# Gated linear attention block: the gates' chain ahead of four silus and of the values' units, an output unit's half made ahead, and the join of the sums of squares inside the last tile

## What is computed

```python
q, k, v, r, lr = jnp.split(hn @ w_in, [...], axis=-1)
gk = jax.nn.log_sigmoid((lr @ w_gate + b_gate)) / GLA_TAU        # TAU = 16
bcum = jnp.cumsum(chunks(padf(gk), GLA_DK), axis=3)
q_dec, k_dec = qf * jnp.exp(bcum), kf * jnp.exp(-bcum)
att = jnp.where(causal, einsum(q_dec, k_dec), 0.0)
chunk_kv = einsum(kf * jnp.exp(b_last - bcum), vf)
o = att @ vf + q_dec @ states
o = rmsnorm(o, g_head) * jax.nn.silu(r)
mix = o @ w_out
h = h + rmsnorm(mix, g[3])
```

## Time and profile before

| | us |
|---|---|
| median of 3 runs (1863.05 to 1868.45) | 1863.25 |
| the profiled execution, its own time | 1867.49 |
| its span in the profile | 1865.7 |
| TensorE busy / weight loads | 1772.6 / 1466.3 |
| VectorE busy | 1092.7 |
| ScalarE busy | 723.7 |
| mean granted TensorE clock | 0.975 of full |

### The profile page before, as it was taken

How to read it: one execution, slowest core, us unless ns; L and a number is a source line. 1 busy time by engine, 2 the same in 40 slices (tenths; PEclk the granted TensorE clock), 3 DMA queues, 4 the chain that set the end, 5 groups by cost and what they waited for, 6 DMA issues and landing times.

```text
span 1865.7 us, 33049 instructions
## 1 busy us (share of the span) xinstructions
PE 1772.6 (95%) x12810; PEld 1466.3 (79%) x12810; DVE 1092.7 (59%) x1981; ACT 723.7 (39%) x1196; POOL 25.1 (1%) x33
## 2 busy tenths in 40 slices
PE   8999998979999999998999999997989999999995
PEld 7999987879999899997899999997954444444442
DVE  4676456578775777669787756868753223232323
ACT  5334453354444544444654446855321111111111
POOL 1000000000000000000000001000002000000000
PEclk8999998989999999999999999998999999999998
DMA  6545422224554355532245545442579999999994
GB/s 222 159 173 200 161 91 94 88 91 158 180 193 168 115 180 183 215 143 91 86 141 182 207 176 190 148 159 91 203 315 416 420 421 420 420 421 420 421 420 200
DMA packets 55534, 409.62 MB, mean 220 GB/s; under 512 B 6432, under 2 KB 6432, under 8 KB 7968
## 3 DMA queue, kind: packets, MB, share of 16 engines
q1 hardware_dynamic: 53424, 401.69, 56.5%
q0 software_dynamic: 1744, 5.79, 1.1%
q10 hardware_dynamic: 288, 1.05, 0.1%
HBM read 405.87 MB, written 2.63 MB: 219 GB/s over the span
## 4 chain that ended last, share of the span: by engine, by line
PE 77%; DVE 11%; DMA 7%; ACT 3%; issue 1%; SPq 0%; DVEq 0%; ACTq 0%
PE ps L565 77%; DMA ring<-w_gate_up 6%; DVE w_lo L1544 1%; ACT moe L1473 1%; PE ps L569 1%; DVE h L1650 1%; DMA raw<-w_units 1%; DVE x_lo L1606 1%; DVE h L1654 1%; DVE arena L1902 1%; DVE rs L1586 1%; DVE arena L1930 0%; ACT w_hi L1167 0%; DVE small L1908 0%; DVE arena L1827 0%
## 5 line engine op out<-in xcount | busy, mean ns | idle before, releaser
L565 PE MATMUL ps<-x_hi,w_hi 128*128 128x256 f32 (+1 forms) x2144 | 622.6, 290 | 17.6 <-DVE x_lo L1604 8.2
L565 PE MATMUL ps<-x_lo,w_hi 128*128 128x256 f32 (+1 forms) x2144 | 616.2, 287 | 0.0
L565 PE MATMUL ps<-x_hi,w_lo 128*128 128x256 f32 (+1 forms) x2144 | 614.2, 286 | 0.0
L1544 DVE TENSOR_TENSOR w_lo<-raw,w_hi 128x1024 fp32r<-128x1024 f32 (+1 forms) x352 | 440.9, 1291 | 86.1 <-ACT w_hi L1167 85.7
L565 PEld LDWEIGHTS ps<-x_hi,w_hi 128*128 128x128 f32 x2144 | 409.5, 191 | 29.1 <-issue 13.7
L1167 ACT ACTIVATE w_hi<-raw 128x1024 fp32r<-128x1024 f32 (+1 forms) x352 | 378.6, 1111 | 110.5 <-PE ps L565 87.2
L565 PEld LDWEIGHTS ps<-x_hi,w_lo 128*128 128x128 f32 x2144 | 411.4, 192 | 0.0
L565 PEld LDWEIGHTS ps<-x_lo,w_hi 128*128 128x128 f32 x2144 | 410.7, 192 | 0.2
L565 PE MATMUL ps<-ring,moe 128*64 128x512 f32 x1536 | 340.4, 595 | 6.4 <-DMA ring<-w_gate_up 4.6
L565 PEld LDWEIGHTS ps<-ring,moe 128*64 128x64 f32 x1536 | 106.0, 137 | 215.8 <-issue 188.6
L565 PE MATMUL ps<-hid_hi,w_hi 128*128 128x272 f32 (+1 forms) x720 | 206.0, 286 | 0.7 <-DVE hid_lo L1606 0.3
(11 more groups left out here) (310 smaller groups left out, 1806.5 us busy)
## 6 DMA issues: line engine op xcount, KB each, us to landing
raw<-w_units SPq DMA_DIRECT2D x144, 1024.0 KB, 4.8
ring<-w_gate_up SPq DMA_DIRECT2D x128, 1024.0 KB, 19.6
ring<-w_down SPq DMA_DIRECT2D x64, 1024.0 KB, 18.4
raw<-w_out_units SPq DMA_DIRECT2D x32, 1408.0 KB, 6.1
bias_rows<-arena POOLq DMA_DIRECT2D x8, 192.0 KB, 3.6
cst<-table SPq DMA_DIRECT2D x1, 1448.0 KB, 12.9
h<-xT SPq DMA_DIRECT2D x1, 1088.0 KB, 5.0
arena<-bias_rows POOLq DMA_DIRECT2D x8, 128.0 KB, 2.5
```

What stands on the lines that cost most here:

```text
L565: return nc.tensor.matmul(out_ap, lhsT, rhs, start=start, stop=stop, skip_group_check=True)
L1544: v.tensor_tensor(part(w_lo, c, 0, n), raw_slot(u, j * n, n), part(w_hi, c, 0, n).bitcast(F32), ALU.subtract).then_inc(lo_made, 1)
```

## The change

Four edits. First, ScalarE makes silus 0 to 3 and the splits up to r's last unit, then the gates' Abs, Exp and Ln; between Ln and the exponentials of the decays stand now the splits of v's first unit, a load of Exp's table and the splits of v's second unit; silus 4 to 7 come after the third exponential, and all other splits after them. Second, on VectorE the chain moves into the loop over r's tiles: min and the subtraction behind the sixth tile, the scans behind the seventh. Third, on ScalarE and VectorE the first half of the output's second unit is made earlier: on ScalarE ahead of `kwT`, on VectorE ahead of the states. Fourth, `project` gets a parameter `within`, called ahead of the seventh of eight parts of the sum in the last tile, and `stat_begin` of `gout` and `sout` is handed over as `within`.

```diff
@@ -606,7 +606,7 @@
                         if k == KT - 1:
                             m.then_inc(full[ts[j][0]], 1)
 
-            def project(u, T, i, src, w, it=0, body=0, kt=KT, n_tiles=2, at=0, x_base=None, between=None):
+            def project(u, T, i, src, w, it=0, body=0, kt=KT, n_tiles=2, at=0, x_base=None, between=None, within=None):
 
                 if x_base is not None and n_tiles == 2:
                     project_as_made(u, T, i, src, w, x_base)
@@ -622,6 +622,8 @@
                         x = slice((at + k) * TA, (at + k) * TA + w)
                         if x_base is not None and j == 0:
                             pe.wait_ge(x_ready, x_base + k + 1)
+                        if within is not None and (j, k) == (n_tiles - 1, kt - 2):
+                            within()
                         first, m = three(bank[:, 0:w], part(w_hi, c, a, P), part(w_lo, c, a, P),
                                          src[0][:, x], src[1][:, x], k == 0, k == kt - 1)
                         if j % (n_tiles // 2) == 0 and k == 0:
@@ -812,7 +814,7 @@
             u0, T = plan["gout"]
             for j in range(4):
                 project(u0 + j, T, 2 * j, X, TA, x_base=None if j else 16,
-                        between=(lambda: stat_begin(3, TA)) if j == 3 else None)
+                        within=(lambda: stat_begin(3, TA)) if j == 3 else None)
             stat_end(3, TA)
             ffn(1, 24, TA, lambda: stat(4, TA))
 
@@ -911,7 +913,7 @@
             u0, T = plan["sout"]
             for j in range(4):
                 project(u0 + j, T, 2 * j, X, SEQ, x_base=None if j else 56,
-                        between=(lambda: stat_begin(9, SEQ)) if j == 3 else None)
+                        within=(lambda: stat_begin(9, SEQ)) if j == 3 else None)
             stat_end(9, SEQ)
             ffn(3, 64, SEQ, lambda: stat(10, SEQ))
 
@@ -1286,11 +1288,16 @@
             root_stat(2, TA, True)
 
 
-            for i in range(8):
+            def r_silu(i):
+
                 t = plan["r"][1].at(i)
-                split_to(plan["r"][0] + i // 2 + 1)
                 act.wait_ge(evac[t[0]], t[1] + 1)
                 nc.scalar.activation(tile(g_r, i, TA), tile(g_r, i, TA), ACT.Silu)
+
+            for i in range(4):
+                split_to(plan["r"][0] + i // 2 + 1)
+                r_silu(i)
+            split_to(plan["r"][0] + 3)
 
             t = plan["gate"].at(3)
             act.wait_ge(evac[t[0]], t[1] + 1)
@@ -1299,12 +1306,17 @@
             did(nc.scalar.activation(g_e1, g_e0, ACT.Exp, scale=-1.0))
             own()
             nc.scalar.activation(g_e2, g_e1, ACT.Ln, bias=C("ones", 0, 1)).then_inc(soft_made, 1)
+            split_to(plan["v"][0])
+            nc.scalar.preload_act_table(ACT.Exp)
+            split_to(plan["v"][0] + 1)
             act.wait_ge(decay_in, 1)
             nc.scalar.activation(g_e0, g_b, ACT.Exp, scale=1.0 / 16).then_inc(decay_made, 1)
             nc.scalar.activation(g_e1, g_b, ACT.Exp, scale=-1.0 / 16).then_inc(decay_made, 1)
             act.wait_ge(decay_in, 2)
             nc.scalar.activation(g_e2, g_e2, ACT.Exp, scale=1.0 / 16).then_inc(decay_made, 1)
-            split_to(plan["gout"][0])
+            for i in range(4, 8):
+                r_silu(i)
+            split_to(plan["gout"][0] + 1, 1)
             for i in range(GH):
                 t = plan["kwT"].at(i)
                 bank = filled(t)
@@ -1741,14 +1753,16 @@
                         t = plan["gate"].at(n)
                         v.tensor_scalar(tile(g_b, n, TA), filled(t)[:, 0:TA], W("b_gate", n, n + 1), None, ALU.add)\
                             .then_inc(evac[t[0]], 1)
-            mine(plan["gate"].at(3))
-
-            dve.wait_ge(soft_made, 1)
-            then(v.tensor_scalar(g_b, g_b, 0.0, None, ALU.min))
-            then(v.tensor_tensor(g_e2, g_b, g_e2, ALU.subtract))
-            for i in range(GH):
-                s = v.tensor_tensor_scan(tile(g_b, i, TA), C("reset_g"), tile(g_e2, i, TA), 0.0, ALU.mult, ALU.add)
-            s.then_inc(decay_in, 1)
+                if i == 5:
+                    mine(plan["gate"].at(3))
+                    dve.wait_ge(soft_made, 1)
+                    then(v.tensor_scalar(g_b, g_b, 0.0, None, ALU.min))
+                    then(v.tensor_tensor(g_e2, g_b, g_e2, ALU.subtract))
+                if i == 6:
+                    for n in range(GH):
+                        e = v.tensor_tensor_scan(tile(g_b, n, TA), C("reset_g"), tile(g_e2, n, TA), 0.0, ALU.mult, ALU.add)
+                    e.then_inc(decay_in, 1)
+
             dve.wait_ge(decay_in, 1)
             b4 = g_b.rearrange("p (h t) -> p h t", h=GH)
             e4 = g_e2.rearrange("p (h t) -> p h t", h=GH)
```

## The result

| | before | after |
|---|---|---|
| median of the runs, us | 1863.25 (5 runs) | 1847.05 (5 runs, 1842.3 to 1851.62) |
| profiled execution, its own time | 1867.49 | 1845.18 |
| span | 1865.7 | 1843.3 |
| mean granted clock | 0.975 | 0.982 |

The ratio after to before is 0.9908 with a 95% interval of 0.9893 to 0.9923, or 17.1 us less. In a later series of runs the same kernel had 1843.51 against 1861.99, ratio 0.9901 (0.9887 to 0.9916). The forecast was 18.4 us less and 1844.9.

What follows compares the result with a forecast made beforehand. The prediction saw the kernel bound by matmul, 77% of the chain that ended last, with time to gain from waiting or slow-clocked matmuls. Terms summed to 18.4 us off the 1863.25 median: 1844.9, range 1840.5 to 1851.

Steps and rivals of the forecast that it cites:

- Gates' chain: Linear attention, values' units: reordered queues remove TensorE's whole stall ahead of the second values' unit, 8.9 us.
- the slack of `soft_made`: VectorE's new wait in the loop over r's tiles: soft_made comes 1.7 us early, so the wait is free.
- Clock behind v: Second values' unit: 22 matmuls return to full clock once the stall ahead is gone, 2.0 us; 0 the other end.
- Half made ahead: Between the first two output units: TensorE's wait for a low half goes, 2.1 us, plus 1.7 for the clock behind.
- Joins: Sums of squares, last tile: the wait for the seventh addition goes, 1.8 us in the output unit, 1.9 in attention.
- The place that I called free by 0.2 us: Attention block: the joining matmuls' new place comes 0.2 us behind the addition, so TensorE barely avoids waiting.
- The table switch: ScalarE's added table load: priced at 1.28 us from the rows, against about 2.66 with a drain from the Trainium skill.
- The sum: All terms, in linear attention and the attention block: 8.9+2.0+2.1+1.7+1.8+1.9 = 18.4 us less.
- the second one: Rival, values' units: a wait takes the stall's place and half returns, about 9 us less gain, 1854; chance 0.06.
- The first one: Rival, TensorE's clock: slow stretches stay or fall elsewhere, leaving 14.7 us gain, 1848.6; chance 0.12.
- The range: Whole kernel: 1851 if clock terms and close places are lost, 1840.5 if another 2.0 us slow stretch vanishes; run differences included.

Runs made afterwards that it cites:

- e5: The changed kernel with VectorE's part of the gates' chain back behind the eighth r tile, ScalarE's order as changed; median 1847.65 us, ratio 0.9915.
- e4: The kernel before with 17 unread products on TensorE between the first and second values' unit, filling the stall; median 1860.98 us, ratio 1.0008.
- e2: The kernel before with only the first half of the second output unit made early; median 1860.56 us, ratio 0.9986.
- e3: The kernel before with only the joins moved inside the last tile; median 1863.53 us, ratio 1.0002.
- e10: e3 plus seven unread products on TensorE in the quiet ahead of the attention's first turned tiles; 1859.56 us, ratio 0.9987.
- e11: e3 unchanged, measured once more; 1864.53 us, ratio 1.0009.
- e1: The kernel before with only the gates' chain moved, on ScalarE and VectorE; median 1852.78 us, ratio 0.9951.
- e7: The changed kernel with the half made ahead taken out again; 1848.97 us (1 run).
- e9: The changed kernel plus seven unread products in each of two quiet stretches, ahead of the first output unit and the attention's first turned tiles; 1844.54 us, ratio 0.9904.
- e6: The changed kernel with eight more Abs on ScalarE ahead of the gates' Exp; median 1861.31 us.

## Why the prediction was right

- **Gates' chain, 8.9 us.** Right. The chain took 6.04 us where 6.05 was counted, the wait for `soft_made` was free, and the slacks at the first three units were 2.2, 3.7 and 6.6 us against 2.0, 3.0 and 4.5. The row that showed less than counted was the slack of `soft_made` itself, 0.7 and not 1.7 us: TensorE's slow stretch at the gates' products was shorter in that execution, and the sixth r tile came earlier. VectorE's move, counted as part of this term, gains nothing (e5).
- **Clock behind v, 2.0 us.** The mechanism is shown (e4). Its size is 1.4 to 2.2 by execution (before, e2, e3, e10, e11), and 2.2 in the one that I counted from. From the start of v's first unit to the first output product, 80.6 us became 69.5: 11.1, against 10.9 for both terms.
- **Half made ahead, 2.1, and 1.7 for the clock.** 13.53 us from the first output unit's first matmul to the second's became 11.45: 2.1. The second output unit took 7.63 to 7.66 us in all seven kernels that kept the idle (before, e1, e3, e4, e7, e10, e11) and 6.01 in those that did not: 1.6 to 1.7. This answers the sentence in which I set the Trainium skill (TensorE: Matmul & The Clock Gate, "What's actually happening") against the row: at this place the fall did not come at another moment, and the term counts. Elsewhere it did: the slow stretches at the gates' products and behind v's stall changed in length, and in the attention stage one changed from 3 to 23 us and another came and went. There what the Trainium skill says of an observation that runs free of the kernel's start fits what the runs show, without being proved by them.
- **Joins, 1.8 and 1.9 us.** From the second output unit to the root 23.45 us became 19.92: 3.5, the 1.8 and the clock. In the attention block exactly 2.0. The place that I called free by 0.2 us was free.
- **The table switch.** The added load starts at 274.18, takes 1.28 us and has the next activation at 275.47 at once behind it; the one at 264.96 is followed by a wait for TensorE alone. The larger figure that I cited from the Trainium skill (ScalarE: Activation LUTs, "What ACT_TABLE_LOAD costs") is not seen here.
- **The sum.** For the linear attention stage 16.5 us were counted; it gained 18.2. Of the rest, 1.5 is the span from the gates' products to v's first unit (17.18 to 15.65), which the change does not touch: the slow stretch there was longer in the profiled execution of before. Without it the edits' places in the two stages add up to 18.7 us (11.1, 2.1, 3.5 and 2.0) against the 18.4 forecast, and the medians came out 16.2 and 18.5 apart in the two series. That the second pair lies so near is partly luck: the attention stage alone can move an execution by up to 8.4 us.
- **The rivals.** In the second one, half the stall returning was priced at about 9 us; half of 8.9 and the 2.0 of the clock behind it would be 6.5. No such wait came. The first one, that slow stretches stay or fall elsewhere, is wrong for the two that were counted, but it has a grain of truth: one fell elsewhere in e7, e9 and e10.
- **The range.** Its lower end counted another slow stretch of 2.0 us as a gain if it vanished. Not every stretch is worth its loss: filling the quiet ahead of the first output unit gave nothing (e9). The uncertainty that mattered was one I had not priced, the attention stage's slow stretch, worth 0 to 8.4 us, more than my whole allowance for what runs differ by.

No version here beats the changed kernel clearly: e5 does the same with less, and e9 differs from it by less than its runs do.

## What to carry to other kernels

Where engines take turns on a stream of work, look at what stands in each queue ahead of the next piece that the bottleneck needs: here one engine's order was worth 10 us, and the other's only slack. Price a stall as the idle plus the slow matmuls behind it, and look for who paces the stretch before counting the second part. When a shift changes nothing in the code of a later stage and its time moves all the same, compare the stages and their granted clock before the medians: the join took 3.9 us of waits out of the trace, and its medians showed no gain.

## What the runs showed of the hardware

Behind the same 3.7 us of quiet in the attention stage TensorE's clock stayed at its lower level for about 3 us in one kernel's profile (after) and for about 23 in others (e5, e6, e11), with TensorE busy nearly all of that time (in e11 24.00 of 24.00 us, clock 0.53). The slow loss was 1.5 to 11.4 us, and what it cost the stage 0 to 8.4 us. Filling the quiet with products that nobody reads removed the stretch, and in both kernels where it was done another one, worth 1.5 us, came in the stage's first output unit. The stretches in the linear attention stage were shorter: the one behind the 8.72 us of idle lasted 4.6 us in before.
